# Both layers' chunk inverses ahead of the score search, in six slices, and the W products six advances sooner

## The reference

```python
# branch A: gated delta rule, chunks (the kernel uses chunks of 128 rows, 4 heads, 4 chunks)
lmat = where(strict, einsum(k_beta, kc) * decay, 0)
tmat = inverse of (eye + lmat)            # per head and chunk
u, w = tmat @ v_beta, tmat @ (k_beta * exp(gc))
def step(state, xs):                      # 4 chunks one after another
    v_new = u_i - w_i @ state
    o     = (q_i * exp(g_i)) @ state + attn @ v_new
    state = state * exp(g_last) + (k_i * exp(g_last - g_i)).T @ v_new
# branch C: sparse attention, per block of 128 queries
score = sum over 4 index heads of wi * relu(qi @ ki.T)
_, idx = top_k(score, 128)                # blocks 1, 2, 3; block 0 needs no search
```

## Time and profile before

| | us |
|---|---|
| median of 3 executions | 1949.36 |
| lowest, highest | 1945.45, 1949.75 |
| profiled execution | 1946.41 |
| its span in the profile | 1944.6 |
| TensorE matmul busy in it | 1930.8 |
| VectorE, ScalarE, GpSimd busy | 1018.0, 888.2, 850.2 |

### The profile page before, as it was taken

One profiled execution on the slowest core, in us unless ns is written; L12 is line 12 of the kernel. 1 busy time (PEld: TensorE's weight loads), 2 busy tenths in 40 slices (PEclk: granted clock), 3 DMA queues, 4 the chain that ended last, 5 costly groups with the idle time before them and its releaser, 6 DMA issues.

```text
span 1944.6 us, 23731 instructions
## 1 busy us (share of the span) xinstructions
PE 1930.8 (99%) x9106; PEld 1532.8 (79%) x9106; DVE 1018.0 (52%) x1832; ACT 888.2 (46%) x1355; POOL 850.2 (44%) x644
## 2 busy tenths in 40 slices
PE   9999999999999999999999999999999999999999
PEld 6878887877788878787877888677766788888887
DVE  5757755555745668766464647575644436101210
ACT  6455553344345455543344355586555344312321
POOL 5545432433445454422434445455322445444443
PEclk9999999999999999999999999999999999999999
DMA  5334542423535235632414545322111332222232
GB/s 202 128 118 131 138 134 80 155 77 124 185 102 177 88 114 148 163 106 71 153 65 141 192 151 163 135 77 98 65 55 55 119 108 87 99 97 98 98 114 71
DMA packets 94575, 227.69 MB, mean 117 GB/s; under 512 B 29976, under 2 KB 33048, under 8 KB 93152
## 3 DMA queue, kind: packets, MB, share of 16 engines
q1 hardware_dynamic: 88768, 223.03, 35.1%
q10 hardware_dynamic: 5696, 3.15, 0.6%
HBM read 194.01 MB, written 24.64 MB: 112 GB/s over the span
## 4 chain that ended last, share of the span: by engine, by line
PE 86%; DVE 7%; DMA 2%; ACT 2%; SPq 1%; issue 1%; POOL 1%; ACTq 0%; DVEq 0%
PE bank L442 85%; DVE kv L376 1%; DVE ER L376 1%; PE bank L446 1%; SPq L371 1%; DMA X<-inverses 1%; DVE scs L401 1%; DMA kv<-blocks 1%; DVE tmp L376 1%; DVE m8s L398 0%; ACT lt L428 0%; DVE lt L386 0%; DVE tmp L386 0%; ACT wh L431 0%; DMA st<-units 0%
## 5 line engine op out<-in xcount | busy, mean ns | idle before, releaser
L376 POOL TENSOR_TENSOR wl<-st,wh 128x512 fp32r<-128x512 f32 x602 | 803.4, 1357 | 1020.2 <-ACT wh L431 1020.1
L442 PE MATMUL bank<-hh,wh 128*128 128x512 f32 x1616 | 651.2, 404 | 1.9 <-ACT hh L428 0.6
L442 PE MATMUL bank<-hh,wl 128*128 128x512 f32 x1616 | 629.2, 390 | 0.0
L442 PE MATMUL bank<-hl,wh 128*128 128x512 f32 x1616 | 628.8, 390 | 0.0
L431 ACT ACTIVATE wh<-st 128x1024 fp32r<-128x1024 f32 (+1 forms) x302 | 316.8, 1049 | 238.3 <-PE bank L442 190.5
L442 PEld LDWEIGHTS bank<-hh,wh 128*128 128x128 f32 x1616 | 303.3, 188 | 90.5 <-issue 26.0
L442 PEld LDWEIGHTS bank<-hl,wh 128*128 128x128 f32 x1616 | 303.6, 188 | 67.2 <-issue 6.9
L442 PEld LDWEIGHTS bank<-hh,wl 128*128 128x128 f32 x1616 | 303.3, 188 | 64.6
L376 DVE TENSOR_TENSOR xt<-xt,bank 128x512 f32<-128x512 f32 x40 | 27.4, 686 | 236.0 <-PE bank L442 236.0
L428 ACT ACTIVATE tmp<-bank 128x512 f32<-128x512 f32 x70 | 41.7, 596 | 158.2 <-PE bank L442 151.5
L442 PE MATMUL bank<-fh,wh 128*128 128x512 f32 x256 | 99.6, 389 | 0.0
(11 more groups left out here) (344 smaller groups left out, 2833.4 us busy)
## 6 DMA issues: line engine op xcount, KB each, us to landing
st<-units SPq DMA_DIRECT2D x300, 512.0 KB, 3.5
gates<-tmp SPq DMA_DIRECT2D x48, 256.0 KB, 2.7
gt<-gates SPq DMA_DIRECT2D x48, 256.0 KB, 3.6
pads<-tmp SPq DMA_DIRECT2D x32, 128.0 KB, 2.7
qk<-tmp SPq DMA_DIRECT2D x16, 256.0 KB, 4.2
x_scratch<-xt SPq DMA_DIRECT2D x2, 2048.0 KB, 8.7
xt<-x_scratch SPq DMA_DIRECT2D x2, 2048.0 KB, 8.2
ph<-phi SPq DMA_DIRECT2D x8, 512.0 KB, 4.7
```

What stands on the lines that cost most here:

```text
L376: return NOTHING if self.e is None else self.e.tensor_tensor(out, a, b, op)
L442: return NOTHING if self.e is None else self.e.matmul(out, lhsT, rhs, start=start, stop=stop, skip_group_check=share)
```

## The change

The constants of the fixed order are changed, and with them the lengths of the empty stretches on ACT and SP. Nothing is computed otherwise.

```diff
-INVERSE, BACK = 21, 11
+INVERSE, BACK = 15, 7
-CUTS = (4, 8, 11, 14, 17, 21, 25)
-SELECT = (8, 12, 3)
+CUTS = (4, 10, 15, 20, 25)
+SELECT = (16, 2, 3)
@@ scalar_program, delta
-            yield from idle(INVERSE - BACK + 6)
+            yield from idle(INVERSE - BACK + 2)
             ac.wait_ge(*at("inv", l, 31))
...
-            yield from idle(BACK - 8)
+            yield from idle(BACK - 4)
@@ sync_program, delta
-            yield from idle(INVERSE - BACK + 2)
+            yield from idle(INVERSE - BACK + 1)
             sp.wait_ge(*at("inv", l, 31))
```

## The result

Four executions of the changed kernel took 1974.88 to 1979.28 us, median 1975.9; four of the kernel before, on the same chip, 1945.45 to 1949.75, median 1948.97. The ratio is 1.0145, 95% interval 1.0127 to 1.0162: 1.45% slower. The forecast was 1976.5, range 1962 to 1989.

The account below looks back on a forecast made before the run. TensorE, 99% busy, was taken as the bound; per layer 9.5 + 2.3 + 0.3 + 1.1 + 1.4 = 14.6 us, 29 for two layers, on a base of 1947.5 gave 1976.5 us, range 1962 to 1989.

Parts of the forecast that it names:

- What bounds the kernel: Whole kernel: TensorE's matmuls fill 99% of the span, so other engines' changes count only through TensorE's waits.
- Part 1, the wait at step 25: Block 1's second score product waits for VectorE's late scaling to free banks 2 and 3: 9.5 us a layer.
- What the wait covers: Inverse's last column, ready near 212, costs nothing under the step-25 wait; without that cover some 2 us.
- Part 2, the wait at W: Products of W wait 3.0 us for X0, issued behind main step 34: +2.3 us a layer.
- Part 3, the end: Uncovered end of the stage: removed waits go to block 3's naked score chain, 17.0 against 16.7 us, +0.3.
- The term of 1.1 for coming back to tiles eight times: Between halves of tiles: eight returns at 0.11 to 0.2 us each add 1.1 us a layer.
- Part 4, the clock: TensorE's idle stretch may halve its clock for one half tile, 2.8 us; middle taken, 1.4 a layer.
- clock falls twice a layer: Rival: clock falls at both waits, one half tile each, 4.2 us a layer over forecast, 1985; chance 0.09.
- Faster: Rival: VectorE scales heads 0 and 1 before step 25 needs the banks, M in by 174; 1942, chance 0.06.
- Short wait: Rival: few VectorE operations stretched and X0 lands fast, 8.3 us a layer, 1964; chance 0.17.
- everything late: Rival: all VectorE operations stretched, 12.7 us, X0 late, +3.7; 20.6 a layer, 1989; chance 0.13.
- no change: Rival: the step-25 wait is short and other gains pay for it; chance 0.05.

Follow-up runs that it names:

- experiment 4: Changed kernel with 40 unread 128x512 matmuls filling TensorE's wait at main step 25: 1987.77 us, ratio 1.0213.
- experiment 2: Kernel before with only the new search order, SELECT = (16, 2, 3): 1959.44 us, ratio 1.006.
- experiment 7: Changed kernel with block 1's products and scaling back at old places, its search kept behind the inverse by eight empty steps (SELECT (8, 2, 3)): 1969.01 us, ratio 1.0116.
- experiment 5: Changed kernel with SP's read of X0 issued two steps sooner: 1975.42 us, ratio 1.015.
- experiment 11: Kernel of experiment 7 with 20 unread 128x512 matmuls in TensorE's 5.1 us wait ahead of row 4's mean product: 1965.41 us, ratio 1.011.
- experiment 3: Changed kernel with SELECT = (14, 4, 3), block 1's products two advances sooner, behind only the first slice of the inverse: 1977.96 us, ratio 1.0146.
- Version 8: Kernel of experiment 7 with W two steps later, ACT's and SP's blocking waits later, block 3's products three advances sooner: 1959.27 us, ratio 1.0065.
- experiment 6: Changed kernel with SELECT = (16, 2, 0), block 3's score products three steps sooner: 1973.0 us, ratio 1.0135.
- experiment 10: Kernel before with SELECT = (8, 12, 0), block 3's products and search three steps sooner: 1952.84 us, ratio 1.0034.
- experiment 1: Changed kernel with the old search order, SELECT = (8, 12, 3): 1980.62 us, ratio 1.0167.

## Why the prediction was right, point by point

**What bounds the kernel** was right: VectorE, ACT and POOL did the same work in about the same busy time, and the whole cost is on TensorE.

**Part 1, the wait at step 25** was right in place, cause and size. Forecast: banks free at 200.2, from an inverse that starts at 181.0, 15.8 us of unstretched work and four stretched operations, 3.5 us. Measured: start at 179.69, four stretched operations, bank 2 free at 198.6 and both at 199.2 (198.70 and 0.48): the start came 1.3 sooner than forecast, the list took 19.5 us where 19.3 were forecast. TensorE lost 9.57 us and 0.7 more in the score product (1.72 in place of 1.04), 10.2 together, and 8.69 and 0.7 in the second layer: 9.8 a layer against a term of 9.5. Of the 0.7 in the score product 0.4 is the slower clock (it took 1.28 in experiment 4 at 1.00), which part 4 counts as well, so the wait by itself is 9.4. Experiment 2 has the same wait without the moved inverse, and experiment 7 takes it away with its order alone.

**What the wait covers** was right in its first half: the last column was forecast at about 212 and came at 211.8, and no wait for ACT appeared. The second half was mis-sized: "with that cover gone it would cost some 2 us". Experiment 7, which is this case, shows 5.1 us, and the slower clock behind it. The sum there followed the transpose with its DMAs and the tile's high and low parts behind ACT's wait; what TensorE waited for was the row's square, which ACT does for the mean product, behind the copy of the inverse (1.09 us), two DMA issues (1.31) and a high part (1.06), and which the sum left out.

**Part 2, the wait at W**: 3.0 taken, 3.03 and 2.73 measured, but by two steps that were both off by 3.6 us and cancel. SP was to issue X0 1.35 us behind the end of main step 34, 4.5 ahead of TensorE's need; it did so at 233.09, only 0.9 ahead of it (TensorE stood ready at 237.06 - 3.03 = 234.03). The prediction took SP's wait for the tanh from a place where ACT had nothing else to do; here ACT's four issues of XT0 lay ahead of it. And the four transfers were in 3.97 us after the first issue (237.06), not 7.5 as taken, nor 8.9 as in the earlier trace rows. The wait is real, but experiment 5, which took it away, brought one of 2.8 us in its place in the first layer.

**Part 3, the end** was right. From the last output product's start to the v tile it took 6.5 us in the second layer (930.09 to 936.56) against 6.7 forecast. In the first it took 7.4 (341.78 to 349.20), and the 0.9 more are the clock: the second score product, behind the same wait of 1.56 us, took 2.92 there and 1.98 in the second layer at a clock of 1.00. The term of 1.1 for coming back to tiles eight times, however, was too large: with all other terms of the first layer taken from rows (9.57 for the wait, 0.7 for the slow score product, 1.5 for the slow tile, 2.4 for the wait at W, 1.5 for the slow products there, 1.0 for the end with its slower clock), 16.7 of the 16.9 us by which the stage grew (111.43 to 333.08 became 110.67 to 349.20) are accounted for, and 0.2 is left for it. Since the end's sum is itself read to some tenths, this says only that the term was well below 1.1.

**Part 4, the clock** is the term that was mis-sized most. It was taken at 1.4 us a layer, half of one fall. It fell at both waits, in both layers: some 2 us at step 25 (1.5 in the tile and 0.4 in the score product; 1.2 and 0.4 in the second layer) and 1.5 at W, 3.5 and 3.1 together. The rival "clock falls twice a layer" had the right mechanism at too high a price: 4.2 over the forecast, some 2 measured. The Trainium skill, TensorE: Matmul & The Clock Gate, part on the clock gate, says that an idle array falls to half its clock; the rows behind 198.70 (0.50) and experiment 11 agree. In the profiled execution it fell a third time, in the end of the first layer's stage and behind it (0.50 from 349.20), which cost 0.9 us inside the stage and 1.4 behind it; in the second layer it did not. The mean clock of the other three executions (0.994 against 0.991) fits one fall less in each. That would explain the 3 us between the profiled execution and the median; their traces are not there to show it.

Between the two profiled spans the change costs 32.9 us where the sum said 29: 16.9 in the first layer's stage and 15.1 in the second's (682.14 to 904.02 became 699.63 to 936.56) against 14.6 forecast for each, and 1.4 between them (the first stage starts 0.8 sooner). The clock took 8.9 us in all where 2.8 were forecast, and the returns to tiles gave part of that back. Between the medians it is 27, since the profiled execution of before was 2.6 us faster than its median and that of after 3.4 slower. So against the medians the sum was 2 us too large, and the base of 1947.5 was 1.5 us under the median of before. The forecast's 0.6 us from the median is luck, as is the cancelling in part 2; the step-25 wait, which is most of the sum, was not.

**Rivals.** "Faster" needed M by 174; it came at 179.7. "Short wait" fell to the four stretched operations and to X0 going out late, "everything late" to POOL standing still with TensorE and to X0 landing fast; "no change" needed the short wait as well.

## What to carry to other kernels

In a kernel whose order is written out, draw for every moved step the list of what each engine has ahead of it, and follow every shared PSUM bank by its number: the waits here came through banks 3 and 6, from users that have nothing to do with the step that was moved. Work that stands ahead of a step which waits for a transfer may be free where it is, and no longer free behind it. Once TensorE is 99% busy, price a new wait of some microseconds as its length plus 1.5 to 3 us for a fall of the clock that follows most of them, and expect the next wait to appear when one is taken away.

## What the runs showed of the hardware

- The clock is a source of spread of its own. Executions of one kernel differ with their mean granted clock: experiment 3, 1967.8 us at 0.997 and 1976.1 to 1981.0 at 0.990 to 0.991; version 7, 1966.16 at 0.997 and 1968.5 to 1971.0 at 0.994. Version 8, all five at 0.997, stays within 2.1 us.
- The clock stood at 0.50 behind waits of 9.57 and 5.12 us, and at 0.61 and 0.62 on the mean of 4 us behind those of 3.03 and 2.73 us. Over all traces, the 19 waits of 3.97 to 12.24 us in the two stages were each followed by slow matmuls. Of the 12 waits of 2.21 to 3.54 us ahead of the products of W nine were; three were not (3.52 and 3.38 us in experiment 3, 2.62 in the second layer of experiment 6: products of 2.02 us at 1.00). Of the 14 waits of 1.56 us in the end of the stage four were, and of the four of 1.92 us in experiment 10 one. So the length of a wait doesn't decide by itself, and what does was not found.
- At the lower level a matmul of 128x512 starts every 0.43 us, at the upper every 0.23. The clock was back at 0.93 in the window from 203 to 208, so slow matmuls cost some 1.5 to 2 us a fall in the changed kernel before the level comes back. In experiment 2, behind 6.31 us, it was 2.8 (197.43 to 202.29 for twelve matmuls, and 0.4 in the score product).
- Two-input operations of VectorE took 1.0 us more (1.41, 1.30, 1.34, 1.33 beside 0.34 to 0.38) only while POOL was making low parts; MAX8 and MATCH_REPLACE8 kept their times. An operation with one tensor was stretched too: `bias<-scs`, 1.35 us at 225.52 in experiment 1 in place of 0.28, with POOL at low parts from 223.78. The Trainium skill, GPSIMD Engine Reference, specification table, names the shared SBUF interface; no run here isolated it.
